# Loads across the first stage border, reordered and merged long convolutions, and expert gate and up weights in units of 768 + 768 columns

## The reference

```python
z = h @ w_in[l]                                  # h: normed, modulated tokens
y = concat(hyena_branch(z[..., :1536]), s5_readout(z[..., 1536:], ...))
x = x + g1 * (y @ w_out[l])
# in hyena_branch, kf = spectra of two learned filters:
y = x1 * long_conv(v, kf[:, 0], hy_bias[0])
return x2 * long_conv(y, kf[:, 1], hy_bias[1])   # long_conv: rfft, product, irfft
# 16 experts, each on its 128 chosen tokens; EXPERT_FF = 2816
ye = (silu(xe @ w_gate[e]) * (xe @ w_up[e])) @ w_down[e]
```

## Time and profile before

| | |
|---|---|
| median of 3 runs | 2510.84 us (2508.46 to 2514.4) |
| the profiled execution's own time | 2506.11 us |
| its span, first to last instruction | 2504.4 us |
| busy: PE, PEld, DVE, ACT, POOL | 93%, 71%, 77%, 53%, 14% |
| moved by DMA | 726.40 MB, mean 290 GB/s over the span |
| `prepare` / `mix` | 0 to 239.5 / 239.5 to 535 us |
| `long_convs` / `output_and_route` / `experts` | 535 to 752 / 752 to 949 / 949 to 2504 us |

### The profile page before, as it was taken

One profiled execution on the slowest core, in us unless ns is written; L12 is line 12 of the kernel. 1 busy time (PEld: TensorE's weight loads), 2 busy tenths in 40 slices (PEclk: granted clock), 3 DMA queues, 4 the chain that ended last, 5 costly groups with the idle time before them and its releaser, 6 DMA issues.

```text
span 2504.4 us, 27973 instructions
## 1 busy us (share of the span) xinstructions
PE 2330.7 (93%) x10978; PEld 1775.9 (71%) x10978; DVE 1940.8 (77%) x1424; ACT 1317.3 (53%) x788; POOL 361.7 (14%) x190
## 2 busy tenths in 40 slices
PE   7887989999988947999999999999999999999997
PEld 2334877853445835888888888888888888888886
DVE  4765799837584467888888888888888888888887
ACT  2123422210023216777777677677677677677766
POOL 0543400000002000012012022022022021021011
PEclk9898999999999967999999999999999999999998
DMA  7657344454432255999999999999999999999997
GB/s 271 226 226 261 123 110 128 138 213 149 151 147 85 85 235 185 379 376 366 374 378 373 366 378 374 372 372 379 370 370 377 374 369 375 379 367 373 378 360 294
DMA packets 199344, 726.40 MB, mean 290 GB/s; under 512 B 14050, under 2 KB 60034, under 8 KB 180277
## 3 DMA queue, kind: packets, MB, share of 16 engines
q1 hardware_dynamic: 190878, 694.03, 73.5%
q0 software_dynamic: 5328, 21.50, 3.1%
q10 hardware_dynamic: 3080, 10.09, 1.1%
HBM read 678.40 MB, written 47.17 MB: 290 GB/s over the span
## 4 chain that ended last, share of the span: by engine, by line
PE 55%; DVE 3%; issue 3%; ACT 1%; DMA 0%; POOL 0%; DVEq 0%; ACTq 0%; PEldq 0%; POOLq 0%
PE psum L2143 14%; PE psum L2130 13%; PE psum L2131 13%; PE psum L2132 13%; DVE w_low L2226 3%; PE psum L2111 2%; ACT x_high L2166 1%; ACT w_high L2162 0%; DVE arena L2240 0%; DMA out<-arena 0%; DVE x_low L2230 0%; DVE arena L2286 0%; DVE arena L2282 0%; POOL out L2091 0%; DVEq L2280 0%
## 5 line engine op out<-in xcount | busy, mean ns | idle before, releaser
L2226 DVE TENSOR_TENSOR w_low<-w_raw,w_high 128x4096 fp32r<-128x4096 f32 (+2 forms) x288 | 1164.1, 4065 | 95.3 <-ACT w_high L2162 95.3
L2162 ACT ACTIVATE w_high<-w_raw 128x4096 fp32r<-128x4096 f32 (+2 forms) x288 | 964.1, 3348 | 467.2 <-PE psum L2132 260.5
L2130 PE MATMUL psum<-w_high,x_high 128*128 128x512 f32 (+1 forms) x1536 | 578.0, 376 | 20.0 <-DVE w_low L2226 17.5
L2131 PE MATMUL psum<-w_low,x_high 128*128 128x512 f32 (+1 forms) x1536 | 573.5, 373 | 0.0
L2132 PE MATMUL psum<-w_high,x_low 128*128 128x512 f32 (+1 forms) x1536 | 571.9, 372 | 0.0
L2130 PEld LDWEIGHTS psum<-w_high,x_high 128*128 128x128 f32 x1536 | 290.0, 189 | 80.9 <-DVE w_low L2226 25.1
L2132 PEld LDWEIGHTS psum<-w_high,x_low 128*128 128x128 f32 x1536 | 289.2, 188 | 52.1
L2131 PEld LDWEIGHTS psum<-w_low,x_high 128*128 128x128 f32 x1536 | 289.7, 189 | 49.7
L2143 PE MATMUL psum<-w_high,a_high 128*128 128x512 f32 x704 | 220.8, 395 | 0.0
L2078 POOL TENSOR_TENSOR arena<-arena 1x1 f32<-1x1 f32 x15 | 63.2, 4214 | 1089.1 <-DVE arena L2282 1089.1
L2143 PE MATMUL psum<-w_low,a_high 128*128 128x512 f32 x704 | 217.3, 390 | 0.0
(11 more groups left out here) (361 smaller groups left out, 2638.9 us busy)
## 6 DMA issues: line engine op xcount, KB each, us to landing
w_raw<-in_ex_w_down SPq DMA_DIRECT2D x80, 2048.0 KB, 9.3
w_raw<-in_ex_w_gate SPq DMA_DIRECT2D x64, 2048.0 KB, 9.9
w_raw<-in_ex_w_up SPq DMA_DIRECT2D x64, 2048.0 KB, 10.5
w_raw<-in_ex_w_gate SPq DMA_DIRECT2D x32, 1536.0 KB, 10.4
w_raw<-in_ex_w_up SPq DMA_DIRECT2D x32, 1536.0 KB, 7.3
arena<-in_mod_w SPq DMA_DIRECT2D x24, 1024.0 KB, 6.2
w_raw<-in_ex_w_down SPq DMA_DIRECT2D x16, 1024.0 KB, 8.2
scratch_spec<-arena SPq DMA_DIRECT2D x8, 1024.0 KB, 10.2
```

The costliest lines, as they stand in the source:

```text
L2130: nc.tensor.matmul(o, xt_h[:, x], h[:, f], start=kk == 0, stop=False)
L2131: nc.tensor.matmul(o, xt_h[:, x], l[:, f], start=False, stop=False)
L2162: nc.scalar.activation(high[n % NHI][:, 0:w], raw[n % NS][:, 0:w], ACT.Copy).then_inc(hi_done, 1)
L2226: nc.vector.tensor_tensor(low[n % NS][:, 0:w], raw[n % NS][:, 0:w], high[n % NHI][:, 0:w].bitcast(F32), ALU.subtract).then_inc(lo_done, 1)
```

## The change

It has three parts. **(1)** Five token tiles and the first chunk of `w_in` are loaded by SP while `prepare` still runs, into slots that stay valid over the border (`token_slots`, `w_in_first`); five kept semaphores are not cleared at the border, and the waits for the last table writes move from the end of `prepare` to the places in `mix` that need them. **(2)** In `long_convs` the inverse products are put in another order over all eight PSUM banks, `combine` works on 1024 and 2048 elements at a time, and the splitting of `w_out` and of the rows moves into `output_and_route`. **(3)** An expert's first chunk has 768 gate and 768 up columns; two contraction tiles of both lie side by side in one unit (1536 columns, three products of 512), the two other chunks have 1024, and the down units run in the order 0, 2, 3, 4, 5, 1. DVE makes the low part of the next expert's unit 1 before it evacuates the output.

The diff, parts (1) and (2):

```diff
+        self.token_slots = [at(first, 4) for first in (112, 116, 120, 124, 192)]
+        self.w_in_first = self.over("p_wraw0", 128, 4, F32).rearrange("p (k n) -> p k n", k=KD)
...
             dft(7)
+            sp.wait_ge(used, NU)
+            for n, xin_slot in enumerate(k.token_slots):
+                src = k.i["x"][0, (n - 2) * P:(n - 1) * P, :] if n >= 2 else k.i["ctx"][0, n * P:(n + 1) * P, :]
+                sp.dma_start(xin_slot, src).then_inc(k.tokens_got[n], 16)
+            c = FIRST_CHUNK
+            sp.dma_start(k.w_in_first, k.i["w_in"].rearrange("l (k p) n -> p (l k) n", p=P)[:, :, c * P:(c + 1) * P]).then_inc(k.first_weights, 16)
             spec_out(2)
             spec_out(3)
-            for s in range(2):
-                sp.wait_ge(sput[s], 64)
             sp.wait_ge(rowput, 128)
...
             quarter(3)
-            act.wait_ge(put_in, 64)
-            act.wait_ge(put_lw, 64)
...
                 scaled(n)
             high_part(0)
+            act.wait_ge(k.tables_in, 64)
+            act.wait_ge(k.local_put, 64)
             high_tile(0)
             high_tile(1)
+            for s in range(2):
+                act.wait_ge(k.spec_put[s], 64)
             scaled(4)
             high_part(1)
...
             def backward(order, n, kks):
                 par, tile = divmod(n, 4)
-                o = ps[:, bank(order, 0) + n % 4, :]
+                o = ps[:, bank(par) + tile, :]
                 e, h = divmod(tile, 2)
...
                 pe.wait_ge(ring[0], loads + 16)
                 pe.wait_ge(ring[1], loads + 32)
                 pe.wait_ge(read, 4 * order + 3)
-                pe.wait_ge(done, 4 * order + 2 + order)
+                pe.wait_ge(done, 4 * order + 2)
                 for n in range(4):
-                    backward(order, n, (order,))
+                    backward(order, n, (0,))
                 pe.wait_ge(done, 4 * order + 3)
                 for n in range(4):
-                    backward(order, n, (1 - order,))
-                pe.wait_ge(done, 4 * order + 4)
-                for n in range(4):
-                    backward(order, n, (2,)).then_inc(inv, 1)
+                    backward(order, n, (1,))
                 pe.wait_ge(ring[2], loads + 32)
                 pe.wait_ge(ring[3], loads + 32)
+                pe.wait_ge(read, 4 * order + 4)
                 for n in range(4, 8):
-                    pe.wait_ge(fin, 8 * order + n - 3)
-                    backward(order, n, (order, 1 - order, 2)).then_inc(inv, 1)
+                    backward(order, n, (0, 1))
+                pe.wait_ge(done, 4 * order + 4)
+                for n in range(8):
+                    backward(order, n, (2,)).then_inc(inv, 1)
...
             act.wait_ge(inv, 12)
             for kk in (3, 0, 1):
-                nc.scalar.activation(k.w_high[kk], k.wo[:, kk, :], ACT.Copy).then_inc(whi, 1)
-            for q in range(4):
-                act.wait_ge(fin, 13 + q)
-                nc.scalar.activation(k.x_high[q], k.x2t[:, q, :], ACT.Copy).then_inc(xhi, 1)
-
...
-                co, so = half[:, f % 2, 0, :], half[:, f % 2, 1, :]
-                re, um, reb, umb = (u[:, i, :] for i in range(4))
-                tt(re, ps[:, b, :], co, ALU.add)
-                tt(umb, ps[:, b, :], co, ALU.subtract)
-                tt(um, ps[:, b + 2, :], so, ALU.add)
-                tt(reb, ps[:, b + 2, :], so, ALU.subtract).then_inc(read, 1)
+                b = bank(f)
+                x, y = u[:, 0:4, :], u[:, 4:8, :]
+                at_two = ps[:, b:b + 4:2, :]
+                tt(x[:, 0:2, :], at_two, half[:, f % 2], ALU.add)
+                tt(x[:, 2:4, :], at_two, half[:, f % 2], ALU.subtract).then_inc(read, 1)
                 dve.wait_ge(read, i + 1)
-                for bar, (a, m) in enumerate(((re, um), (reb, umb))):
-                    kre, kim = k.spec[:, 2 * bar, f, :], k.spec[:, 2 * bar + 1, f, :]
-                    t0, t1, t2, t3 = (u[:, 4 + i, :] for i in range(4))
-                    tt(t0, a, kre, ALU.mult)
-                    tt(t1, m, kim, ALU.mult)
-                    tt(t2, m, kre, ALU.mult)
-                    link(tt(t3, a, kim, ALU.mult))
-                    tt(a, t0, t1, ALU.add)
-                    link(tt(m, t2, t3, ALU.subtract))
+                shape = [P, 2, 2, 512]
+                bars = lambda w: w.rearrange("p (b w) c -> p b w c", b=2)
+                kre, kim = (k.spec[:, n:4:2, f, :].unsqueeze(2).to_broadcast(shape) for n in range(2))
+                tt(bars(y), bars(x), kre, ALU.mult)
+                link(tt(bars(x), bars(x), kim, ALU.mult))
+                tt(y[:, 0:4:3, :], y[:, 0:4:3, :], x[:, 1:3, :], ALU.add)
+                link(tt(y[:, 1:3, :], y[:, 1:3, :], x[:, 0:4:3, :], ALU.subtract))
...
                     to = gm if f == 0 else g[:, 1, f - 2]
-                    tt(to[:, 0, :], re, umb, ALU.add)
-                    tt(to[:, 1, :], um, reb, ALU.add)
-                    tt(to[:, 2, :], re, umb, ALU.subtract)
-                    tt(to[:, 3, :], um, reb, ALU.subtract).then_inc(done, 1)
+                    tt(to[:, 0:2, :], y[:, 0:2, :], y[:, 2:4, :], ALU.add)
+                    tt(to[:, 2:4, :], y[:, 0:2, :], y[:, 2:4, :], ALU.subtract).then_inc(done, 1)
...
-                    last = nc.vector.scalar_tensor_tensor(gm[:, a, :], m, -root, gm[:, a, :], ALU.mult, ALU.add)
-                last.then_inc(done, 1)
+                tt(x[:, 0:2, :], y[:, 0:4:2, :], y[:, 1:4:2, :], ALU.add)
+                link(tt(x[:, 2:4, :], y[:, 0:4:2, :], y[:, 1:4:2, :], ALU.subtract))
+                tt(y[:, 0:2, :], x[:, 0:4:2, :], x[:, 1:4:2, :], ALU.add)
+                link(tt(y[:, 3:1:-1, :], x[:, 0:4:3, :], x[:, 1:3, :], ALU.subtract))
+                link(nc.vector.scalar_tensor_tensor(gp, y, root, gm, ALU.mult, ALU.add))
+                nc.vector.scalar_tensor_tensor(gm, y, -root, gm, ALU.mult, ALU.add).then_inc(done, 1)
...
-            for i, kk in enumerate((3, 0, 1)):
-                low_weights(i, kk)
-            gated(4)
-            gated(5)
-            low_rows(0)
-            gated(6)
-            low_rows(1)
-            gated(7)
-            low_rows(2)
-            low_rows(3)
+            for n in range(4, 8):
...
             nc.scalar.activation(w_high[2], wo[:, 2, :], ACT.Copy).then_inc(whi, 1)
+            for q in range(4):
+                nc.scalar.activation(x_high[q], k.x2t[:, q, :], ACT.Copy).then_inc(xhi, 1)
...
+            pe.wait_ge(wlo_first, 3)
+            pe.wait_ge(xlo, 4)
...
+            for kk in (3, 0, 1):
+                nc.vector.tensor_tensor(w_low[kk], wo[:, kk, :], w_high[kk].bitcast(F32), ALU.subtract).then_inc(wlo_first, 1)
+            for q in range(4):
+                dve.wait_ge(xhi, q + 1)
+                nc.vector.tensor_tensor(x_low[q], k.x2t[:, q, :], x_high[q].bitcast(F32), ALU.subtract).then_inc(xlo, 1)
```

Part (3):

```diff
-    chunks = [(0, 1024), (1024, 1024), (2048, FF - 2048)]
...
+    chunks = [(0, 768), (768, 1024), (1792, 1024)]
...
-    tiles = [min(4, FF // P - 4 * d) for d in range(-(-FF // 512))]
+    tiles = [4, 2, 4, 4, 4, 4]
+    first_tile = [0, 4, 6, 10, 14, 18]
+    down_order = [0, 2, 3, 4, 5, 1]
...
+        if n < 4:
+            dst = self.raw[s][:, 0:w].rearrange("p (k h f) -> p k h f", k=2, h=2)
+            for h in range(2):
+                src = self.gate_up[h][0, bass.ds(e, 1), :, 2 * n:2 * n + 2, 0:self.chunks[0][1]].rearrange("e p k f -> p (e k) f")
+                eng.dma_start(dst[:, :, h, :], src).then_inc(self.got[s], 16)
+            return
...
+    gate = lambda c: flat[:, 512:512 + 768] if c == 0 else two(0, 1024)
+    up_of = lambda c: flat[:, 512 + 768:2048] if c == 0 else two(2, 1024)
...
-                    if n < DOWN:
-                        c, up, w = n // 4, n % 4 // 2, chunks[n // 4][1]
-                        if c and n % 2 == 0:
+                    if n < 4:
+                        for kl in range(2):
+                            kk = 2 * n + kl
+                            x = slice(kk * P, (kk + 1) * P)
+                            for b in range(3):
+                                f = slice(kl * 1536 + 512 * b, kl * 1536 + 512 * (b + 1))
+                                o = ps[:, 1 + b, :]
+                                nc.tensor.matmul(o, xt_h[:, x], h[:, f], start=kk == 0, stop=False)
+                                nc.tensor.matmul(o, xt_h[:, x], l[:, f], start=False, stop=False)
+                                last = nc.tensor.matmul(o, xt_l[:, x], h[:, f], start=False, stop=kk == KD - 1)
+                    elif n < DOWN:
+                        c, up = n // 4, n % 4 // 2
+                        if n % 2 == 0 and n > 4:
                             pe.wait_ge(amul if up else silu, e * NCW + c)
-                        for kl in range(KH):
-                            kk = KH * (n % 2) + kl
-                            x = slice(kk * P, (kk + 1) * P)
-                            for b in range(2):
```

(19 more changed lines are left out.)

126 lines of the change are left out of this document (57 added, 69 removed).

## The result

The changed kernel takes 2451.68 us (median of 4 runs, 2443.13 to 2455.14) against 2510.43 us: a ratio of 0.9759, 95% interval 0.9728 to 0.979.

What follows compares the result with a forecast made beforehand. Bounds: a barrier with a load behind it, the order of products, and TensorE's own stream with DMA close beside it. 8.6 + 20.3 + 16 = 44.9 us off 2506.1 gave 2461.2, plus 4.7 for the median; forecast 2465, range 2455 to 2481.

Steps and rivals of the forecast that it cites:

- Border: Between `prepare` and `mix`: first tile scaled at 234.8 instead of 243.44, moved waits hidden; 8.6 us less.
- Order of the long convolutions: `long_convs`: reordered inverse products remove TensorE's waits for combines and the slow clock behind them; 20.3 us less.
- rival D: `long_convs`: merged instructions slower than their elements, 8 to 17 us lost, about 2477; chance 0.06.
- Moved splitting: Border behind `long_convs`: splitting hides beside 32 products; clock gain between 0 and 2.4 us, taken as 0.
- (a): Experts: products of 512 replace those of 512 and 256; 0.4 us less an expert.
- (b): Start of an expert: smaller unit 0 parts shorten TensorE's wait; 0.9 us less, bounds 0 and 1.15, 15 times.
- (c): Experts: new tight places at unit 4's parts and DVE's units 1 and 2; costs 0.1 us an expert.
- (d): Experts: weight loads asked for at shorter distance, wanted 12.3 us after issue instead of 16; costs 0.15 us an expert.
- A: Experts: transfers become the bound, so product and wait savings buy nothing; 2482, chance 0.13.
- B: Expert's start: the wait is replaced by one for unit 1, 2 or 4; 2477, chance 0.12.
- C: Experts: four extra transfers each add a fixed part, slower than before; 2642, chance 0.04.
- E: Border before `mix`: early loads or moved waits take back most of 8.6 us; 2473, chance 0.05.

Runs made afterwards that it cites:

- e1: Part (1) of the change alone, on the kernel before: 2501.05 us, ratio 0.9956.
- e2: Part (2) of the change alone, on the kernel before: 2486.14 us, ratio 0.9906.
- e3: Part (3) of the change alone, on the kernel before: 2487.54 us, ratio 0.9907.
- e13: Kernel before, with only the low part of the next expert's unit 1 made ahead of the evacuation: 2510.62 us, ratio 0.9993.
- e0: The changed kernel run again without an edit: 2452.7 us, ratio 0.9763.
- e9: Changed kernel with the old `combine` of 20 instructions of 512 elements: 2450.93 us, ratio 0.9757.
- e8: Changed kernel with the splitting of `w_out` and of the rows back at the end of `long_convs`: 2460.65 us, ratio 0.9807.
- e5: Changed kernel with first-chunk gate and up columns in separate units again (products of 512 and 256, one transfer per unit): 2473.07 us, ratio 0.9843.
- e4: Changed kernel with the low part of the next expert's unit 1 back behind the evacuation: 2470.2 us, ratio 0.9835.
- e6: Changed kernel with nine more transfers in each expert, data not used: 2485.39 us, ratio 0.9895.
- e10: Changed kernel with each contraction tile in `output_and_route` waiting for itself, not for the last low part: 2452.61 us, ratio 0.9763.
- e12: e10 with each token tile's transposes and router products one product group later: 2442.81 us, ratio 0.9724.
- e11: e10 plus six products that nobody reads in each of two TensorE pauses: 2451.98 us, ratio 0.9773.

## Why the prediction was wrong

The terms, against what the profiles show: the mean of four without the part, less the mean of four with it (before, e1, e2, e3, e13 as far as they lack it; the changed kernel's three and the part alone; three without part (3), since e13 changes the experts):

| term | forecast | measured |
|---|---|---|
| border, tables to first fp32r product | 8.6 | 26.0 - 16.7 = 9.3 |
| `long_convs` | 20.3 | 217.7 - 196.6 = 21.2 |
| clock behind its border | 0 (0 to 2.4) | 29.3 - 27.1 = 2.1 |
| experts | 16 | 1528.2 - 1502.9 = 25.3 |
| sum | 44.9 | 57.9 |

The sum agrees with the medians (58.8 us).

- **Border**: right, in mechanism and nearly in size. One step was off: the tables were to land 5.2 us after their issue and the moved waits to be hidden; they landed after 8.0 us, and ACT stood 0.93 us. That is small against the gain, and e0's profile does not have the wait.
- **Order of the long convolutions**: right step by step. Order 0's 48 tile products took 41.36 us (41.3 forecast), the stage ended 21 us earlier, combine 2 was in time. DVE's last gating follows TensorE's last product by 1.2 us.
- **Merged combines**: right, nothing that can be seen (e9). The 2048-element instructions took 2.28 us, so rival D fell.
- **Moved splitting**: I counted the cost behind the border at nothing, which held, and the clock at nothing, which did not: with the shorter pause it stayed up, 2.1 us in the mean, in eleven of the twelve profiles with this border. I had written the bound (2.4) and taken its low end. What I had not seen is that with the new order this edit carries 9.3 us, 6.7 of pause and 2.6 behind it (e8); the forecast held that gain in its "20.3" only because it worked with the end of the gating.
- **Experts**: this is the step that failed, by 9.3 of the 13 us. The mechanism was right; the sizes were not. (a) Products: 0.30 us an expert instead of 0.4 (e5), a little less. (b) The wait, the term that failed most: I took 0.9 and bounded it by its idle time, 1.15. The rows price it at 1.4 from start to start, and 1.65 us of period less 0.30 leave 1.35. e4 and e13 show that both edits are needed for it, the smaller unit 0 and the early low part of unit 1, and that together they leave TensorE nothing to wait for. (c) and (d) The tight places and the bursts of loads were charged with 0.25 us, 4 us in all, and cost nothing: the profile after shows no wait of TensorE, although loads land after 7.6 to 17.6 us, later than the 12.3 that (d) reckoned with, and ACT waits 4.1 us for them. 1.35 + 0.30 against 1.05 is 0.6 us for each of 16 experts.

Of the rivals, A (transfers as the bound) did not occur, though 6.6% more bytes (e6) are past the point where it begins; B would be e4; C (e5, without the four transfers, is no faster), D and E fell. One sign that I had named misled: ACT waiting for `w_raw` was to mean A or C, and it does wait, but TensorE does not feel it. The range failed at its lower end. The bounds that I had written for single terms (15 x 0.25 of (b), 16 x 0.25 of (c) and (d), 2.4 of the clock, 0.5 of the border) add up to 10.7 us, all on one side, so 2455 was where all of them come true together. They nearly did; beyond them (b) brought 3 us more (15 x 0.2) and the convolutions 0.9, and (a) took back 1.6.

## What to carry to other kernels

A place that is "just in time" by 0.1 us costs nothing until it is late, and its price then is more than its idle time (1.04 us for a wait of 0.77 in e4): take it from start to start. Keep such a place as a bound and do not charge it as an average. When an expected wait goes, ask for every edit that holds it away, because a second one may carry much of it (the early low part here, the moved splitting in the convolutions). A wait of one engine that is moved by a few us should be followed to the next engine's chain at once: e10 gained nothing until e12 moved the transposes too.

## What was not expected of the hardware

- Executions of the same kernel differ by up to 15 us although an expert takes 93.80 us to 0.05 in every one. About half of it is in `prepare`, where the mean granted clock of the same 20 us was 1.00 or 0.72; why it fell in one execution and not in the other stays open.
- 256 columns in fp32r cost more than half of 512: 24 products more for the same columns cost 0.30 us, 12 ns each (e5).
- A wait costs more than its idle time: 0.77 us of idle time took 1.04 us out of the stream, 1.15 took 1.4.
- DMA ran at 406 GB/s over a whole expert with eighteen more transfers, and 380 GB/s at a busy share of 0.97 still left TensorE without a wait: the busy share alone did not say how far away the bound was.
- A clock that six added products had brought up fell again 1 us into the next stream of products, behind a wait of 2.46 us (e11).
